# The gates of the last quarter of experts: through a grid in DRAM instead of one-hot products

## The chip, the cores and the metric

The kernel runs on one core of one Trainium2 chip. The metric is the device time of one launch in microseconds. The five engines of the core have queues of their own and wait for each other by semaphores: TensorE (PE, with its weight loads PEld), VectorE (DVE), ScalarE (ACT), GpSimd (POOL) and SyncE (SP), whose queue issues most of the DMAs. DMAs are carried out by 16 DMA engines. SBUF is the memory on the core, PSUM the banks that matmuls write to, DRAM the large memory outside.

## The reference

A decoder of two layers on 256 tokens of width 1024. Each layer has a token mixer (a short convolution in the first, latent attention in the second) and then a PEER mixer, which picks 16 of 16,384 experts for each token and each of 8 heads:

```python
s = einsum("chpd,hpnd->chpn", q, subkeys); top_s, top_i = top_k(s, 16)
cand = top_s[:, :, 0, :, None] + top_s[:, :, 1, None, :]
best_s, best_pos = top_k(cand.reshape(C, 8, 256), 16)
ia = take_along_axis(top_i[:, :, 0], best_pos // 16); ib = take_along_axis(top_i[:, :, 1], best_pos % 16)
expert = ia * 128 + ib
g = softmax(best_s)
act = gelu(einsum("chkd,cd->chk", u_tab[expert], xc)) * g
return einsum("chk,chkd->cd", act, v_tab[expert])
```

An expert has two numbers, ia (first key) and ib (second key), each from 0 to 127. A token has 8 x 16 = 128 chosen experts with a gate g each; two heads may choose the same expert, and then their gates add.

## The kernel before, in words

The kernel gathers no tables. For every expert it computes the product with u for all tokens, and multiplies the gelu by a dense grid of gates, which is zero where a token did not choose the expert. A panel is the 128 experts of one first key: 128 x 1024 values of u or v, 512 KB. There are 128 u panels and 128 v panels in each layer. Products are in split fp32: ScalarE converts a landed panel (`raw`, four slots) to its high part `w_hi` (L944), VectorE (in the selection GpSimd) computes the low part `w_lo` (L1321, L1277), and TensorE multiplies both.

The stages of `peer(l)`: RMS norm (ScalarE's root is L963); the selection, in which VectorE finds the chosen experts while TensorE runs 16 query panels and 6 u panels; "ahead", 26 u panels (j = 0 to 25); "mix", three loops (q = 0, 1, 2) of 8 iterations, each with 4 u panels of the next quarter of first keys and 4 v panels of quarter q; "last", the 32 v panels of the last quarter.

The gates come to the grid by one-hot products. In ahead, `turn(t)` (j = 11 and 13) brings the chosen numbers of each token to lie across partitions; ScalarE copies them to `ia_t`, `ib_t` and the gates to `g32_t`. For 16 tokens at a time VectorE then makes one-hots of the second key (L1538) and of 32 first keys (L1542), multiplies the latter by the high and low halves of the gates (L1547), and TensorE multiplies them token by token into a bank [second key x 32 first keys] (L643, `scatter_side`; L655, `scatter`, in ahead). ScalarE and VectorE bring the result to `arena` (L1015, L1557). Quarter 0 is scattered in ahead, quarters 1, 2 and 3 in the three loops of mix: one group of 16 tokens in each half body. `arena` holds two quarters of the grid, quarter q in half q mod 2. `weigh` (L1572) multiplies gelus by gates for two experts' panels at a time; its semaphore is `w_mul`.

The order of each engine's work is the order of the code. SyncE's queue loads panels: a load waits until the low part of the panel four before is computed (`lo_done`), so the queue is at most four panels ahead. In the first layer GpSimd's queue loads the 56 last rows of the modulation weights (`ada1`, L1301), one at a time, each after VectorE has used the one before (L1347).

Of the kernel before, what the change touches and what calls it, by code (L numbers as in the profile page):

```python
# [20 lines left out]
F32 = mybir.dt.float32  # L21
# [38 lines left out]
SCATTER = 13  # L60
FIRST = KEYS // 8
# [48 lines left out]
def program(nc, xT_in, c_in, pos_in, vec_in, con_in, ada_in, pan_in, key_in, iota_in, u_in, v_in, out):  # L110
    ctx = ExitStack()
    with ctx:
# [80 lines left out]
        smax = sb("smax", [P, 3, 2])  # L193
        ssum = sb("ssum", [P, 3, 2])
        gqk = sb("gqk", [P, 1])[:]
# [12 lines left out]
        eq = [arena[:, a:a + SEL * TOPK].bitcast(BF16) for a in (13312, 3584)]  # L208
        g_high, g_low = [arena[:, a:a + T // 2].bitcast(F16) for a in (6144, 6144 + T // 2)]
# [52 lines left out]
        ada_seen = sem("ada_slot_seen_free")  # L262
# [96 lines left out]
        def _(sp):  # L359
# [16 lines left out]
            def load_experts(l):  # L376
                k0 = KEYS * l
                for i, (kind, n) in enumerate(SEARCH):
                    load(*((pan_in, DENSE[f"peer_q{l}"] + n) if kind == "q" else (u_in, k0 + n)), f"sel{l}", i)
                if l == 0:  # L380
                    sp.dma_start(con[:, C_MASK:C_N], con_in[:, C_MASK:C_N]).then_inc(s_iota, 16)
                    sp.dma_start(iota_w, iota_in).then_inc(s_iota, 16)
                for j in range(AHEAD - EARLY):
                    load(u_in, k0 + EARLY + j, f"ahead{l}", j)
                for q in range(3):
                    with sp.Fori(0, 8) as it:
                        for e in range(4):
                            v = k0 + q * QUART + e
                            load(u_in, it * 4 + (v + AHEAD), f"mix{l}", 64 * q + 2 * e, 8, it)
                            load(v_in, it * 4 + v, f"mix{l}", 64 * q + 2 * e + 1, 8, it)  # L390
                for first in (0, 4):
                    with sp.Fori(first, first + 4) as it:
                        for j in range(4):
                            load(v_in, it * 4 + (k0 + 3 * QUART + j), f"last{l}", j, 4, it)
                    if l == 0 and first == 0:
                        sp.wait_ge(g_done, 2 + 64)
                        sp.dma_start(posi, pos_in.partition_broadcast(P)).then_inc(s_pos, 16)
# [49 lines left out]
        def _(pe):  # L447
# [211 lines left out]
            def peer(l):  # L659
# [33 lines left out]

                for j in range(AHEAD - EARLY):
                    if j in TURN:
                        turn(TURN.index(j))
                    u_panel(l, f"ahead{l}", j, len(SEARCH) + 1 + j, PAN[j % 2])
                    for g in groups_after(j) if j >= SCATTER else ():
                        if g == 1:
                            pe.wait_ge(idx_copied, TT * (l + 1))  # L700
                        scatter(l, g % 2, 64 * l + g + 1)
                for n in range(4):
                    pe.matmul(YB[n][:], zero[:], act_hi[:, 0:512], start=True, stop=False, skip_group_check=True)
                for q in range(3):
                    with pe.Fori(0, 8) as it:
                        for s in range(2):
# [5 lines left out]
                            scatter_side(l, s, it * 2 + (64 * l + 16 * (q + 1) + s + 1))  # L712
# [225 lines left out]
        def _(act):  # L938
# [84 lines left out]
            def peer(l):  # L1023
                rms_of(2 * l + 2)
# [25 lines left out]

                for j in range(AHEAD - EARLY):
                    if j in TURN:
                        turned(TURN.index(j))
                    split_hi(f"ahead{l}", j + HI_LEAD)
# [11 lines left out]
                    for g in groups_after(j) if j >= SCATTER else ():  # L1066
                        copy_gates(0, g % 2, 64 * l + g + 1, g * GT)
# [5 lines left out]
                def mix_body(q, it, end):  # L1073
                        for s in range(2):
# [10 lines left out]
                            copy_first(q + 1, it * 2 + (64 * l + 16 * (q + 1) + s + 1), (it * 2 + s) * GT)  # L1085
# [182 lines left out]
        def _(pool):  # L1268
# [16 lines left out]

            pool.wait_ge(s_const, 48)
# [8 lines left out]
            for j in range(KB):  # L1295
                split_lo("conv_out", j)
            select_panels(0)
            with pool.Fori(0, 96 - ADA_FIRST) as it:
                pool.wait_ge(ada1_used, it + 1)
                pool.sem_inc(ada_seen, 1)  # L1300
                pool.dma_start(ada1[:], ada_in[bass.ds(it + ADA_FIRST, 1)].rearrange("o p n -> p (o n)")  # L1301
                               ).then_inc(ada1_landed, 16)
# [8 lines left out]
            select_panels(1)  # L1311


        @block.vector
        def _(dve):
# [290 lines left out]
            def experts(l):  # L1606
                for j in range(SCATTER, AHEAD - EARLY):
                    for g in groups_after(j):
                        if g % (P // GT) == 0:
                            dve.wait_ge(idx_copied, TT * l + g // (P // GT) + 1)  # L1610
                        second_key_hots(g % 2, 64 * l + g + 1, g * GT)
# [6 lines left out]
                weigh(0, 0, 64 * l + 16 + 2)  # L1618
                split_weighted(0, 64 * l + 1)

                def mix_body(q, it, end):
                    for s in range(2):
# [3 lines left out]
                        second_key_hots(s, it * 2 + (64 * l + 16 * (q + 1) + s + 1), token0)  # L1626
# [10 lines left out]
                        if not (end and s):  # L1637
                            weigh(it * 4 + (2 * s + 2), it * 4 + (q % 2 * QUART + 2 * s + 2), 64 * l + 16 * (q + 1) + 2)
                        split_lo(f"mix{l}", j + 4, 8, it)
                        sum_products(it * 4 + (96 * l + 32 * q + 2 * s + 2), PAN[1], it * 4 + (2 * s + 1))  # L1640
                        add_gates(q + 1, it * 2 + (48 * l + 16 * q + s + 1), token0)
# [16 lines left out]
                def last_body(it, end):  # L1658
                    for s in range(2):
                        split_lo(f"last{l}", 2 * s + 1, 4, it)  # L1660
                        if not (end and s):
                            weigh(it * 4 + (2 * s + 2), it * 4 + (QUART + 2 * s + 2), 64 * l + 64 + 2)
# [369 lines left out]
```

## Time and profile before

| | us |
|---|---|
| median of 3 runs | 1899.36 (1897.52 to 1900.22) |
| the profiled execution, its own time | 1898.04 |
| its span, first to last instruction | 1896.4 |
| TensorE busy | 1879.8 |
| VectorE busy | 1579.3 |
| ScalarE busy | 1023.6 |
| GpSimd busy | 308.3 |

The span is that of one profiled execution; its own time is the span and 1.6 us around it. Busy times of matmuls are modelled, so the chain of waits is read beside them: it goes back from the last instruction to what released each step. In the first layer mix begins at about 299 us and the third loop at about 672; in the second layer the same places lie some 948 us later. HBM is read at 195 GB/s over the span, and 1.05 MB are written.

### The profile page before, as it was taken

The numbers are of one execution on the slowest core, as the hardware profiler recorded it, in microseconds if no ns is written. First come the engines' busy times: TensorE is split into PE (matmuls) and PEld (weight loads), VectorE is DVE, ScalarE is ACT, GpSimd is POOL, SyncE is SP. The second block draws the span as 40 slices with busy tenths as digits, with TensorE's granted clock in tenths as the row PEclk, the third lists the DMA queues.
The fourth block names the chain that finished last, engine by engine and source line by source line (L and its number), as shares of the span: only waits on it lengthen the run. The fifth ranks groups of instructions, "written<-read, shape, count | busy, mean of one in ns | idle before, by whom it ended". The sixth has DMA issues, their size and how long they took to land.

```text
span 1896.4 us, 39962 instructions
## 1 busy us (share of the span) xinstructions
PE 1879.8 (99%) x13150; PEld 1667.1 (88%) x13150; DVE 1579.3 (83%) x3083; ACT 1023.6 (54%) x1658; POOL 308.3 (16%) x177
## 2 busy tenths in 40 slices
PE   9999999999999999999999999999999999999999
PEld 8999998888888888887889999988888888888887
DVE  6758999999999999997765489988888888888866
ACT  4354555555555555554455545555555555555553
POOL 3877500000000000000063574000000000000000
PEclk8999999999999999999999999999999999999999
DMA  9965646777777767777732355456556556556564
GB/s 360 365 209 163 199 133 188 225 229 226 220 228 226 231 224 227 224 229 228 230 107 89 129 161 168 134 169 182 182 177 182 183 179 183 181 179 185 178 191 141
DMA packets 104153, 371.77 MB, mean 196 GB/s; under 512 B 11393, under 2 KB 13825, under 8 KB 103681
## 3 DMA queue, kind: packets, MB, share of 16 engines
q1 hardware_dynamic: 96000, 341.26, 56.7%
q0 software_dynamic: 8064, 29.36, 5.1%
q8 instruction: 52, 0.85, 0.2%
q14 instruction: 37, 0.30, 0.1%
HBM read 369.53 MB, written 1.05 MB: 195 GB/s over the span
## 4 chain that ended last, share of the span: by engine, by line
PE 90%; DVE 5%; ACT 1%; DMA 1%; DVEq 1%; issue 1%; POOL 1%; SPq 0%; ACTq 0%; POOLq 0%
PE bank L624 36%; PE bank L609 17%; PE bank L614 9%; PE bank L588 5%; PE bank L593 5%; PE bank L589 5%; PE bank L643 2%; PE bank L655 1%; DVE w_lo L1321 1%; POOL w_lo L1277 1%; PE bank L671 1%; PE bank L885 1%; DVE arena L1407 1%; PE bank L453 1%; DVE arena L1448 1%
## 5 line engine op out<-in xcount | busy, mean ns | idle before, releaser
L944 ACT CAST w_hi<-raw 128x1024 fp32r<-128x1024 f32 (+1 forms) x603 | 631.2, 1047 | 324.1 <-DMA raw<-in_v_panels 129.4
L1321 DVE TENSOR_TENSOR w_lo<-raw,w_hi 128x1024 fp32r<-128x1024 f32 x488 | 596.8, 1223 | 119.4 <-PE bank L624 52.3
L609 PE MATMUL bank<-act_two,w_hi 128*128 128x512 f32 x1536 | 379.3, 389 | 0.0
L609 PEld LDWEIGHTS bank<-act_two,w_hi 128*128 128x128 f32 x1536 | 288.3, 188 | 59.8
L624 PE MATMUL bank<-w_hi,wt_hi 128*128 128x512 f32 x1024 | 328.0, 401 | 1.4 <-DVE wt_lo L1583 0.8
L624 PE MATMUL bank<-w_lo,wt_hi 128*128 128x512 f32 x1024 | 318.1, 391 | 0.0
L624 PE MATMUL bank<-w_hi,wt_lo 128*128 128x512 f32 x1024 | 317.1, 390 | 0.0
L1277 POOL TENSOR_TENSOR w_lo<-raw,w_hi 128x1024 fp32r<-128x1024 f32 (+2 forms) x115 | 273.6, 2382 | 150.2 <-PE bank L593 54.8
L588 PE MATMUL bank<-act_two,w_hi 128*128 128x256 f32 x984 | 246.1, 288 | 0.0
L589 PE MATMUL bank<-act_two,w_hi 128*128 128x256 f32 x984 | 241.2, 283 | 0.0
L624 PEld LDWEIGHTS bank<-w_hi,wt_lo 128*128 128x128 f32 x1024 | 192.3, 188 | 42.1
L624 PEld LDWEIGHTS bank<-w_lo,wt_hi 128*128 128x128 f32 x1024 | 192.2, 188 | 41.7
L614 PEld LDWEIGHTS bank<-act_two,w_lo 128*128 128x128 f32 x1536 | 209.5, 190 | 15.0
L614 PE MATMUL bank<-act_two,w_lo 128*128 128x256 f32 x1536 | 213.8, 282 | 0.0
L997 ACT COPY ring_g<-bank 128x256 f32 (+1 forms) x192 | 71.7, 374 | 253.9 <-PE bank L614 253.8
L624 PEld LDWEIGHTS bank<-w_hi,wt_hi 128*128 128x128 f32 x1024 | 177.8, 189 | 31.3 <-DVE w_lo L1321 3.6
L589 PEld LDWEIGHTS bank<-act_two,w_hi 128*128 128x128 f32 x984 | 188.5, 192 | 0.0
L588 PEld LDWEIGHTS bank<-act_two,w_hi 128*128 128x128 f32 x984 | 188.2, 191 | 0.0
L1538 DVE TENSOR_TENSOR hot_b<-ib_t,iota 128x2048 bf16<-128x2048 bf16 x128 | 156.0, 1219 | 0.3 <-PE bank L655 0.2
L1301 POOL DMA_DIRECT2D ada<-in_ada_rows x56 | 29.9, 534 | 688.1 <-DVE ada_sum L1347 688.1
L593 PE MATMUL bank<-act_two,w_lo 128*128 128x256 f32 x984 | 138.5, 283 | 0.0
L593 PEld LDWEIGHTS bank<-act_two,w_lo 128*128 128x128 f32 x984 | 127.2, 192 | 0.0
(249 smaller groups left out, 2057.5 us busy)
## 6 DMA issues: line engine op xcount, KB each, us to landing
raw<-in_u_panels SPq DMA_DIRECT2D x256, 512.0 KB, 3.7
raw<-in_v_panels SPq DMA_DIRECT2D x256, 512.0 KB, 3.7
raw<-in_panels SPq DMA_DIRECT2D x81, 512.0 KB, 4.0
ada<-in_ada_rows POOLq DMA_DIRECT2D x56, 512.0 KB, 4.8
arena<-in_ada_rows SPq DMA_DIRECT2D x40, 512.0 KB, 6.6
raw<-in_panels SPq DMA_DIRECT2D x6, 384.0 KB, 3.1
arena<-in_subkeys SPq DMA_DIRECT2D x2, 1024.0 KB, 6.4
xT<-in_xT SPq DMA_DIRECT2D x1, 1024.0 KB, 7.1
```

The costliest lines, as they stand in the source:

```text
L588: pe.matmul(bank, w_hi[:, hi_slot, w], acts[0][k], start=(k == 0), stop=False)
L589: pe.matmul(bank, w_hi[:, hi_slot, w], acts[1][k], start=False, stop=False)
L593: mm = pe.matmul(bank, w_lo[:, lo_slot, w], acts[0][k], start=False, stop=(k == KB - 1))
L609: pe.matmul(bank[:, 0:2 * T], w_hi[:, hi_slot, w], act_two[:, :, a], start=(k == 0), stop=False, skip_group_check=True)
L614: mm = pe.matmul(bank[:, 0:T], w_lo[:, lo_slot, w], act_hi[:, a], start=False, stop=(k == KB - 1), skip_group_check=True)
L624: mm = pe.matmul(YB[2 * t + n][:], wt[:, par, a], (w_hi, w_lo)[v][:, slots[v], n * 512:(n + 1) * 512], start=False, stop=False, skip_group ...
L643: mm = pe.matmul(GB[t // (GT // 2)][:, o:o + 2 * QUART], hb[:, t, :], hg[:, t, :], start=True, stop=True)
L944: nc.scalar.copy(w_hi[:, slot, 0:width], raw[:, slot, 0:width]).then_inc(hi_done, 1)
L997: nc.scalar.copy(ring_g[:, bass.ds(slot * T, T)], bank[:, T:2 * T]).then_inc(lo_copied, 1)
L1277: pool.tensor_tensor(w_lo[:, lo_slot, 0:width], raw[:, slot, 0:width], w_hi[:, slot, 0:width].bitcast(F32), ALU.subtract).then_inc(lo_done, 1)
L1321: dve.tensor_tensor(w_lo[:, lo_slot, 0:width], raw[:, slot, 0:width], w_hi[:, slot, 0:width].bitcast(F32), ALU.subtract).then_inc(lo_done, 1)
L1538: dve.tensor_tensor(wide(hot_b[:, par, :]), each(ib_t, KEYS, token0), numbers(0, KEYS), ALU.is_equal)
```

## The change

The three loops keep quarters 1 and 2 as they are; the one-hots, the scattering, the copies and additions of quarter 3 in the third loop are gone. In their place:

- A grid in DRAM for each layer, 16,384 experts x 256 tokens in fp32. At the start of `peer` ScalarE's queue writes zeros over its last quarter (4.19 MB).
- At j = 15 (`BACK`) of ahead, `turn_back` on TensorE brings ia and ib back to one token a partition, four matmuls; ScalarE (`row_starts`) computes 256 x ib + token and stores the scaled gates in `g32_t`, and VectorE adds 256 x 128 x ia, which gives `place`, the position in the grid.
- GpSimd adds the gates to the grid: one indirect DMA for each of 2 x 8 x 16 columns of `place`, 128 single elements each, with a wait after each head's 32. The gates of all quarters are sent, those of the first three to a part of the grid that nobody reads.
- SyncE waits for the last head's additions ahead of iteration 4 of the third loop, and then loads the last quarter of the grid to `arena` in eight pieces of 512 KB, two ahead of each of the last four iterations' panel loads. VectorE waits for them at the end of the third loop (`s_grid`).
- The 56 rows `ada1` are loaded by SyncE's queue, between panel loads.
- Counts of the semaphores for one-hots and gates follow; `smax`, `ssum` and `gqk` lie in `place`.

```diff
+BACK = 15
@@ sync
+                def load_ada1(it, n):
+                    if l == 0:
+                        sp.wait_ge(ada1_used, it + (n + 1))
+                        sp.dma_start(ada1[:], ada_in[bass.ds(it + (n + ADA_FIRST), 1)].rearrange("o p n -> p (o n)")
+                                     ).then_inc(ada1_landed, 16)
+                def mix_loads(q, it):
+                    for e in range(4):
+                        v = k0 + q * QUART + e
+                        load(u_in, it * 4 + (v + AHEAD), f"mix{l}", 64 * q + 2 * e, 8, it)
+                        load(v_in, it * 4 + v, f"mix{l}", 64 * q + 2 * e + 1, 8, it)
+                        if e % 2:
+                            load_ada1(it * 2, 16 * q + e // 2)
+                def load_grid(n):
+                    a = 3 * QUART + 4 * n
+                    sp.dma_start(arena[:, (QUART + 4 * n) * T:(QUART + 4 * n + 4) * T].rearrange("p (a t) -> p a t", t=T),
+                                 grid[l][a * KEYS * T:(a + 4) * KEYS * T].rearrange("(a p t) o -> p a (t o)", p=P, t=T)
+                                 ).then_inc(s_grid, 16)
-                for q in range(3):
+                for q in range(2):
                     with sp.Fori(0, 8) as it:
...
+                        mix_loads(q, it)
+                with sp.Fori(0, 4) as it:
+                    mix_loads(2, it)
+                sp.wait_ge(added[HEADS - 1], 16 * TT * TOPK * (l + 1))
+                sp.wait_ge(w_mul, 64 * l + 32)
+                for g in range(4):
+                    load_grid(2 * g)
+                    load_grid(2 * g + 1)
+                    mix_loads(2, 4 + g)
@@ tensor
+                def turn_back():
+                    pe.wait_ge(idx_copied, TT * (l + 1))
+                    for n, numbers in enumerate((ia_t, ib_t)):
+                        for t in range(TT):
+                            by_rank = numbers[:, t * P * DUP:(t + 1) * P * DUP].rearrange("p (t r) -> p t r", r=DUP)[:, :, 0]
+                            mm = pe.matmul(SC[0][:, (n * TT + t) * P:(n * TT + t + 1) * P], by_rank, ident_b[:], start=True,
+                                           stop=True)
+                    mm.then_inc(back_done, 1)
...
+                pe.wait_ge(place_ready, l + 1)
...
-                            scatter_side(l, s, it * 2 + (64 * l + 16 * (q + 1) + s + 1))
+                            if q < 2:
+                                scatter_side(l, s, it * 2 + (48 * l + 16 * (q + 1) + s + 1))
@@ scalar
             def peer(l):
+                nc.scalar.dma_start(grid[l][3 * QUART * KEYS * T:KEYS * KEYS * T].rearrange("(p c t) o -> p c (t o)", p=P, t=P),
+                                    zero[:].bitcast(F32).unsqueeze(1).broadcast_to([P, 2 * QUART, P])).then_inc(s_zero, 16)
                 rms_of(2 * l + 2)
...
+                def row_starts():
+                    act.wait_ge(tokens_ready, 1)
+                    act.wait_ge(back_done, l + 1)
+                    for t in range(TT):
+                        i = nc.scalar.activation(row_start[:, t * P:(t + 1) * P], SC[0][:, (TT + t) * P:(TT + t + 1) * P],
+                                                 ACT.Identity, bias=tok[:, t:t + 1], scale=float(T))
+                    i.then_inc(start_ready, 1)
+                    nc.scalar.mul(g32_t[:], gate.rearrange("p t n -> p (t n)"), G_SCALE).then_inc(gates_kept, 1)
@@ gpsimd
+            def add_gates_by_dma(l):
+                pool.wait_ge(s_zero, 16 * (l + 1))
+                pool.wait_ge(place_ready, l + 1)
+                pool.wait_ge(gates_kept, l + 1)
+                for h in range(HEADS):
+                    for t in range(TT):
+                        for k in range(TOPK):
+                            n = t * SEL + h * TOPK + k
+                            pool.indirect_dma_start(grid[l], bass.IndirectOffsetOnAxis(place[:, n:n + 1], 0), g32_t[:, n:n + 1], None,
+                                                    compute_op=ALU.add).then_inc(added[h], 16)
+                    pool.wait_ge(added[h], 16 * TT * TOPK * (l + 1))
@@ vector
+                    if j == BACK:
+                        dve.wait_ge(start_ready, l + 1)
+                        i = dve.scalar_tensor_tensor(out=place[:], in0=SC[0][:, 0:TT * P], scalar=float(KEYS * T),
+                                                     in1=row_start, op0=ALU.mult, op1=ALU.add)
+                        i.then_inc(place_ready, 1)
...
                         if end and s:
+                            if q == 2:
+                                dve.wait_ge(s_grid, 128 * (l + 1))
                             weigh_part(most, (q + 1) % 2 * QUART, w_most)
-                        first_key_hots(q + 1, s, token0)
+                        if q < 2:
+                            first_key_hots(q + 1, s, token0)
```

SyncE's queue at the end of the third loop's rolled part, before the change (first layer; L364 is a panel load, L386 the loop's end, and then come the loads of the last stage):

```order
L364 DMA raw<-in_u_panels 128x1024
L363 REGISTER_ALU
L364 ISA [waits panel_lo_ready]
L364 DMA raw<-in_v_panels 128x1024
L386 REGISTER_ALU
L386 COMPARE_AND_BRANCH
```

And after the change, where the rolled part ends with iteration 3 (L375 is a panel load, L400 an ada row, L414 a piece of the grid):

```order
L375 DMA raw<-in_v_panels 128x1024
L399 REGISTER_ALU
L400 ISA [waits ada1_used]
L400 DMA ada<-in_ada_rows 128x1024
L421 REGISTER_ALU
L421 COMPARE_AND_BRANCH
L414 DMA arena<-gates_by_expert 128x4x256 [waits weighted_gelu_ready,gates_of_head7_added]
L414 DMA arena<-gates_by_expert 128x4x256
L375 DMA raw<-in_u_panels 128x1024 [waits panel_lo_ready]
```

The wait for the additions of all heads now stands ahead of the panel loads of the last four iterations, and two pieces of the grid ahead of each.

GpSimd's queue between the selection of the first layer and the attention's panels, before (L1277 is a low part, L1301 the load of an ada row):

```order
L1277 TENSOR_TENSOR w_lo<-raw,w_hi 128x1024 [waits panel_multiplied,panel_hi_ready] x24
L1298 UNCONDITIONAL_BRANCH
L1298 ISA
L1301 ISA [waits ada1_used]
L1301 DMA ada<-in_ada_rows 128x1024
L1298 REGISTER_ALU
L1298 COMPARE_AND_BRANCH
L1277 TENSOR_TENSOR w_lo<-raw,w_hi 128x1024 [waits panel_multiplied,panel_hi_ready,panel_lo_ready]
```

And after (L1345 is a low part, L1375 one of the additions; the groups of heads 1 to 6 are left out):

```order
L1345 TENSOR_TENSOR w_lo<-raw,w_hi 128x1024 [waits panel_multiplied,panel_hi_ready] x24
L1375 DMA gates_by_expert<-g_t,place 4194304x1 [waits scaled_gates_kept,gate_places_ready,gate_grid_zeroed]
L1375 DMA gates_by_expert<-g_t,place 4194304x1 x31
...
L1375 DMA gates_by_expert<-g_t,place 4194304x1 [waits gates_of_head6_added]
L1375 DMA gates_by_expert<-g_t,place 4194304x1 x31
L1345 TENSOR_TENSOR w_lo<-raw,w_hi 128x1024 [waits panel_hi_ready,panel_multiplied,panel_lo_ready,gates_of_head7_added]
```

A loop of one waiting load has become eight groups of 32 additions, each group behind the landing of the one before.

## Rows read from the trace of the kernel before

**Rows 1.** The page, parts 1 and 2: busy time, 40 slices.
```profile
span 1896.4 us, 39962 instructions
PE 1879.8 (99%) x13150; PEld 1667.1 (88%) x13150; DVE 1579.3 (83%) x3083; ACT 1023.6 (54%) x1658; POOL 308.3 (16%) x177
...
PEclk8999999999999999999999999999999999999999
DMA  9965646777777767777732355456556556556564
GB/s 360 365 209 163 199 133 188 225 229 226 220 228 226 231 224 227 224 229 228 230 107 89 129 161 168 134 169 182 182 177 182 183 179 183 181 179 185 178 191 141
```

**Rows 2.** Chain of waits, 670 to 720 us: start, length, engine, tile, line, number.
```profile
by line: PE bank L624 49.7%; PE bank L609 31.7%; PE bank L614 15.2%; PE bank L643 3.9%
...
680.72 0.48 PE bank L643 x16
681.20 2.83 PE bank L624 x12
...
686.79 2.75 PE bank L624 x12
```

**Rows 3.** Busy time by stretch; its columns are in the first line.
```profile
core 0: us, PE busy (x) PEld busy (x) DVE busy (x) ACT busy (x) POOL busy (x), PEclk, DMA share, GB/s
...
670.00:856.00 186.00, 186.00 (x1155) 159.34 (x1154) 172.60 (x269) 106.40 (x178) 8.48 (x16) 1.00 0.72 226
...
1618.00:1804.00 186.00, 186.00 (x1156) 159.25 (x1155) 155.81 (x227) 105.51 (x178) 0.00 (x0) 1.00 0.59 181
```

**Rows 4.** Timeline, first layer: start, length, engine, line, operation, shapes.
```profile
245.21 2.22 PE L689 MATMUL bank<-ident_b,arena 128*128 128x128 bf16 x32
...
255.51 1.05 ACT L944 CAST w_hi<-raw 128x1024 fp32r<-128x1024 f32 x1
...
255.92 1.22 DVE L1321 TENSOR_TENSOR w_lo<-raw,w_hi 128x1024 fp32r<-128x1024 f32 x1
```

**Rows 5.** Timeline, third loop: a load's issue and its panel's first product.
```profile
752.57 0.33 SPq L364 DMA_DIRECT2D raw<-in_u_panels  x1
...
764.97 1.98 PE L609 MATMUL bank<-act_two,w_hi 128*128 128x512 f32 x8
```

**Rows 6.** Lines L1301, L1277, L1448: instructions, shortest/median/longest ns, starts, forms.
```profile
L1301 POOL DMA_DIRECT2D ada<-in_ada_rows x56: 530/530/722, 219.6 to 937.1; - x56
...
L1277 POOL TENSOR_TENSOR w_lo<-raw,w_hi x115: 1270/2404/3812, 27.5 to 1163.1; 128x1024 fp32r<-128x1024 f32 x105, 128x768 fp32r<-128x768 f32 x6, 128x512 fp32r<-128x512 f32 x4
...
L1448 DVE TENSOR_TENSOR arena<-arena x64: 159/191/2422, 148.3 to 1162.8; 128x32 f32<-128x32 f32 x32, 128x48 f32<-128x48 f32 x16, 128x16 f32<-128x16 f32 x16
```

**Rows 7.** Timeline, selection: GpSimd, and VectorE beside it.
```profile
155.56 2.41 POOL L1277 TENSOR_TENSOR w_lo<-raw,w_hi 128x1024 fp32r<-128x1024 f32 x1 [0.48 <-PE bank L593]
...
156.80 1.53 DVE L1448 TENSOR_TENSOR arena<-arena 128x32 f32<-128x32 f32 x4
```

**Rows 8.** Lines L442, then L364: DMA issue ns, and landing.
```profile
L442 SPq DMA_DIRECT2D out<-xT x4: 372/383/400, 1889.9 to 1893.6; - x4
...
DMA to landing us min/median/max: 2.3/2.3/2.4
...
L364 SPq DMA_DIRECT2D raw<-in_u_panels x256: 327/333/343, 127.5 to 1783.2; - x128
...
DMA to landing us min/median/max: 2.5/3.7/9.4
```

**Rows 9.** Timeline, start of peer in the first layer.
```profile
130.01 0.27 ACT L963 ACTIVATE ring_g<-bank,eps 128x2 f32<-128x2 f32 x1 [1.21 <-PE bank L555]
...
130.38 0.33 SPq L364 DMA_DIRECT2D raw<-in_panels  x1
```

**Rows 10.** Waits, 670 to 856 us: us in total, times, longest.
```profile
ACT w_hi L944 <- DMA raw<-in_v_panels: 23.8, 15, 2.1
```

**Rows 11.** The page, part 3: packets, MB, share of 16 engines.
```profile
q0 software_dynamic: 8064, 29.36, 5.1%
```

More of the change, by code:

```diff
@@ L111, in program @@
     ctx = ExitStack()
+    grid = [nc.dram_tensor(f"gates_by_expert{l}", (KEYS * KEYS * T, 1), F32, kind="Internal").ap() for l in range(2)]
     with ctx:
@@ L192, in program @@
         lat = act32[:, 512:512 + 5 * T]
-        smax = sb("smax", [P, 3, 2])
-        ssum = sb("ssum", [P, 3, 2])
-        gqk = sb("gqk", [P, 1])[:]
+        place = sb("place", [P, TT * SEL], I32)
+        tok = sb("tok", [P, TT])
+        smax, ssum = [place[:, 6 * i:6 * i + 6].bitcast(F32).rearrange("p (e t) -> p e t", e=3) for i in range(2)]
+        gqk = place[:, 12:13].bitcast(F32)
         topv = arena[:, 0:TT * 2 * TOPK]
@@ L261, in program @@
         ada1_used = sem("ada1_used")
-        ada_seen = sem("ada_slot_seen_free")
+        tokens_ready = sem("token_numbers_ready")
+        back_done = sem("expert_numbers_turned_back")
+        start_ready = sem("row_starts_ready")
+        place_ready = sem("gate_places_ready")
+        gates_kept = sem("scaled_gates_kept")
+        s_zero = sem("gate_grid_zeroed")
+        added = [sem(f"gates_of_head{h}_added") for h in range(HEADS)]
+        s_grid = sem("last_quarter_of_gates_landed")
         s_silu = sem("silu_c_ready")
@@ L384, in load_experts @@
                     load(u_in, k0 + EARLY + j, f"ahead{l}", j)
-                for q in range(3):
-                    with sp.Fori(0, 8) as it:
[L387 to L390, printed above, removed]
+                def load_ada1(it, n):
[16 more added lines that the diff above has]
+                for q in range(2):
+                    with sp.Fori(0, 8) as it:
+                        mix_loads(q, it)
[7 more added lines that the diff above has]
+                    mix_loads(2, 4 + g)
                 for first in (0, 4):
@@ L394, in load_experts @@
                             load(v_in, it * 4 + (k0 + 3 * QUART + j), f"last{l}", j, 4, it)
+                        load_ada1(it, 48)
                     if l == 0 and first == 0:
-                        sp.wait_ge(g_done, 2 + 64)
+                        sp.wait_ge(g_done, 2 + 48)
                         sp.dma_start(posi, pos_in.partition_broadcast(P)).then_inc(s_pos, 16)
@@ L696, in peer @@
                         turn(TURN.index(j))
+                    if j == BACK:
+                        turn_back()
                     u_panel(l, f"ahead{l}", j, len(SEARCH) + 1 + j, PAN[j % 2])
@@ L1053, in peer @@
                         turned(TURN.index(j))
+                    if j == BACK:
+                        row_starts()
                     split_hi(f"ahead{l}", j + HI_LEAD)
@@ L1284, in select_panels @@
                     split_lo(f"ahead{l}", j)
+            pool.iota(tok[:], [[P, TT]], 0, 1, allow_small_or_imprecise_dtypes=True).then_inc(tokens_ready, 1)
             pool.wait_ge(s_const, 48)
@@ L1296, in _ @@
                 split_lo("conv_out", j)
-            select_panels(0)
[L1298 to L1302, printed above, removed]
+            def add_gates_by_dma(l):
[9 more added lines that the diff above has]
+                    pool.wait_ge(added[h], 16 * TT * TOPK * (l + 1))
+            select_panels(0)
+            add_gates_by_dma(0)
             pool.wait_ge(lo_done, ring("last0", 31)[3] + RAW)
@@ L1311, in _ @@
             select_panels(1)
+            add_gates_by_dma(1)
         @block.vector
@@ L1625, in mix_body @@
                         split_lo(f"mix{l}", j + 1, 8, it)
-                        second_key_hots(s, it * 2 + (64 * l + 16 * (q + 1) + s + 1), token0)
+                        if q < 2:
+                            second_key_hots(s, it * 2 + (48 * l + 16 * (q + 1) + s + 1), token0)
                         split_lo(f"mix{l}", j + 2, 8, it)
```

20 lines of the change are left out of this document (12 added, 8 removed).

## The prediction

> **What bounds the kernel now.** I read the page first: in a span of 1896.4 us TensorE is busy for 1879.8, at the full clock in all slices but the first; VectorE has 83% [rows 1]. Next the chain of waits in the third loop of the first layer: it never leaves TensorE, and one group of it, L643, is the scattering that the change removes there [rows 2]. The busy time of the third loops says how near the others are: TensorE 186.0 of 186 us in both layers, VectorE 172.6 in the first and 155.8 in the second, DMA engines 0.72 and 0.59 [rows 3]. So TensorE time that is removed in this loop shortens the span one for one, work taken off VectorE and ScalarE there earns nothing, and what is added elsewhere is free until it holds TensorE.
>
> **What is removed.** Each half body of the third loop holds one scatter_side of 16 matmuls. It takes 0.48 us on the chain, and the twelve matmuls behind it take 2.83 us where those not behind one take 2.75 [rows 2]: 0.56 us each. Two layers of 16 make 32, so -17.9 us. The 16 sets of one-hots, gate copies and additions of each layer go too. Nothing is late in their place: TensorE's next wait, for the split panel, is served by a VectorE that has more room than before.
>
> **What is added, step by step.**
> - TensorE: turn_back, four 128x128 bf16 matmuls per layer. The 32 of a turn took 2.22 us [rows 4], so 0.28 us, and with a change of bank 0.35: +0.7 us for both layers.
> - ScalarE: two activations and a multiplication, about 1 us, put ahead of the conversion at 255.51. VectorE: one operation of 256 columns, at most 0.6 us, behind the split at 255.92 [rows 4]. That split serves a panel whose low part TensorE multiplies some 3 us later, so both hide. I take 0; without cover 1.6 us a layer.
> - The zeroing: 4.19 MB written from ScalarE's queue at the start of peer, in runs of 512 bytes. ScalarE idles there for 1.21 us before L963, and SyncE's next load is at 130.38 [rows 9]. The nearest rows are the output stores, also runs of 512 bytes: 383 ns of issue, 2.3 us to landing for 256 KB [rows 8]. At an issue of that size the step is free. I take 0. The other end is the whole transfer: at the 365 GB/s of the second slice [rows 1] 11.5 us, by sixteen stores 37 us.
> - The additions, 256 indirect transfers a layer in eight groups, each group with a wait for its landing. They may start when VectorE has written place, at about 257.2 + 0.6 = 258 us [rows 4]. SyncE waits for the last group ahead of the load that stands at 752.57, whose panel TensorE multiplies at 764.97 [rows 5]. That leaves 495 us. The eight landings at 2.3 us each [rows 8] cost 18, so a transfer may take 1.86 us. The trace has no indirect one. The lower end is GpSimd's plain DMA, 0.53 us, which also has 128 pieces; the upper is GpSimd's longest kind of instruction, 2.40 us at the median [rows 6]. The kind is that of the lower row, but 128 positions must be read and an element added, so I take 1.4: 258 + 256 x 1.4 + 18 = 634 us, and the wait on SyncE is met long before it is reached. Nothing on GpSimd stands behind them that is due earlier, since its next split waits for the end of the last loop.
> - The ada rows move from GpSimd's queue to SyncE's. SyncE would wait there for one VectorE operation that directly follows the split which released the load before, and the load after it needs a later split still. So 0; without that cover each panel load behind a row would come later by that one operation, which its 6 us of room (below) take up.
> - The fetch of the grid: eight loads of 512 KB within four iterations, two at a time ahead of a panel load. Two take 1.05 MB / 365 GB/s = 2.9 us [rows 1]. A panel load has 12.4 us from issue to use [rows 5], of which landing, conversion and split take 3.7 + 1.05 + 1.22 [rows 4, 8]; 6.4 us remain. ScalarE already waits up to 2.1 us for landings without TensorE waiting [rows 10]. I take +1 us for both layers, bounds 0 and 8 x 2.9 = 23.
>
> Sum, against the profiled execution, which took 1898.0 us: 1898.0 - 17.9 + 0.7 + 1.0 = 1881.8. The median of the runs shown is 1.3 us above that execution, so I predict 1883.
>
> **Two rules weighed.** VectorE's L1448 ran 0.16 us at best and 2.42 at worst; its four instructions from 156.80 took 1.53 us because the first waited for a GpSimd instruction that read SBUF until 157.97 [rows 6, 7]. The lock on the shared port is real in this kernel. GpSimd's plain DMAs, issued while VectorE was 92% busy, took 530 ns at the median and 722 at most [rows 6]. The Trainium skill (SBUF — State Buffer, "Who interferes with whom") says that a VectorE instruction with two SBUF inputs contends with a GpSimd instruction that reads SBUF, and that descriptor writing is stopped only by two-port modes. The trace agrees with both; what it cannot show is whether fetching 128 positions counts as a read. It is rival D.
> The Trainium skill (Perfetto Trace Analysis, "DMA Instruction — HWDGE") says that the sequencer is free for its next instruction only after all descriptors of its DMA have been generated, and that a full buffer makes the DMA engines start before that. The trace bears the first half out only at small sizes: 512 pieces cost the queue 383 ns where 128 cost 333 [rows 8]. By the rule the zeroing with 8192 pieces could hold ScalarE; that is rival B.
>
> **Rivals.**
> - A, the additions are late (slower). Place: SyncE's wait in the third loop, behind which stand all panel loads, so TensorE stops when its four panels are used up. It decides from 1.86 us a transfer. The price is 2 x 256 x (x - 1.86): at 2.0 us 72, time 1955; at 2.40, 276, time 2159. For it: nothing in the trace shows an indirect transfer, and each also reads and writes HBM. Against it: 3.5 times the plain DMA would be needed.
> - B, the zeroing holds ScalarE (slower, or no change). ScalarE's root at 130.01 is on TensorE's path, since the norm waits for it. Price 11.5 - 1.2 = 10.3 us a layer, 1883 + 21 = 1904; half of it 1893; at the store's pace 37, 1954.
> - C, the small pieces take the DMA engines. A layer has 32,768 of them, 2048 for each engine. If each took what the mean packet of GpSimd's queue took, 5.1% of 16 x 1896 us over 8064 packets = 192 ns [rows 11], that is 393 us in a window in which 0.72 of 495 is taken: 749 us of work, up to 254 late in the first layer, 190 in the second, about 2330. Against it: that packet carries 4 KB. At half, 96 ns, the sum is 553 and 489 us, 58 late in the first layer only: 1941.
> - D, the additions hold VectorE. In the first layer it has 13.4 us to spare in 186 [rows 3], 26 over the additions' 360 us. If each transfer held it 0.3 us, 77 us, then 51 would show in the first layer and nothing in the second: 1934.
> - E, nothing is gained: the removed blocks were cover for a wait. Time 1899. Against it: the chain has no other engine in it there.
>
> **Chances.** A measurement of this kernel tells a change from none at about 0.2%, 3.8 us. Forecast 0.54, with its own range 1879 to 1890; A 0.12; B 0.15; C 0.09; D 0.05; E 0.05. Faster takes the forecast and a little of B that is only partly held: 0.57. Same takes E and some of B: 0.09. Slower is the rest: 0.34. The range: below 1878 I leave 0.03, and above 1942 about 0.15, which are most of A and the upper part of C. So 1878 to 1942.
>
> **What would show each step.** Right: no L643 in the third loops, each half body 11.0 us in place of 11.6; the 256 transfers start near 258 us and end before 750; SyncE does not wait for them; ScalarE's root at the start of peer comes as soon after TensorE's sums as before. Wrong by A: GpSimd still issuing after 752 us and an idle TensorE in the third loop. By B: TensorE idle at the start of peer, with ScalarE's DMA issue long. By C: panel landings well above 3.7 us and DMA share near 1 from 258 us on. By D: VectorE's instructions longer than their 1.22 and 0.69 us in the first two loops. If TensorE is busy throughout and the time is still above 1890, the removed blocks were worth less than the 0.56 us that I read.

## The result, and the profile after it

The changed kernel takes 2059.53 us (median of 4 runs, 2054.01 to 2063.39), the kernel before 1899.65 in the same comparison: 1.0842 times as long, 95% interval 1.0814 to 1.0869. It is slower by 160 us, where 1883 was forecast. The profiled execution took 2057.83 us with a span of 2056.0.

The page of the changed kernel, to be held against [rows 1]:

```profile
span 2056.0 us, 38401 instructions
PE 1871.7 (91%) x12646; PEld 1659.1 (81%) x12646; DVE 1490.9 (73%) x2893; ACT 1002.0 (49%) x1600; POOL 1239.4 (60%) x634
...
PE   9999999999999980899999999999999999406999
...
POOL 4877288887888887000162772888888888881000
PEclk9999999999999995999999999999999999757999
...
q0 software_dynamic: 73728, 0.29, 8.3%
```

TensorE has fewer busy microseconds than before and yet a share of 91%, because it stands still in two places, slice 16 and slices 35 to 37. They lie in the middle of the two third loops, where the panels of iteration 4 are due. GpSimd is busy with additions up to these places. The waits of TensorE (engine, who it waited for, us in total, times, longest) put a figure on them:

```profile
PE bank L648 <- ACT w_hi L997: 166.4, 2, 98.8
PE bank L512 <- ACT act_two L1024: 2.2, 3, 1.7
```

So 67.6 us in the first layer and 98.8 in the second, and nothing else of size. Behind ScalarE's conversion stands a panel that SyncE had not asked for. SyncE's own queue (start, duration of the issue) in the first layer shows why, beside the last two transfers on GpSimd:

```profile
745.81 0.33 SPq L375 DMA_DIRECT2D raw<-in_v_panels  x1
746.96 0.33 SPq L400 DMA_DIRECT2D ada<-in_ada_rows  x1
820.24 0.94 SPq L414 DMA_DIRECT2D arena<-gates_by_expert  x2
821.24 0.50 SPq L375 DMA_DIRECT2D raw<-in_u_panels  x1
...
815.36 1.55 POOL L1375 DMA_INDIRECT gates_by_expert<-g_t,place  x1 [0.30 <-issue]
817.21 1.55 POOL L1375 DMA_INDIRECT gates_by_expert<-g_t,place  x1 [0.31 <-issue]
```

The panel load that stood at 752.57 before [rows 5] now goes out at 821.24. SyncE goes on 3.0 us after the start of the last addition (817.21 to 820.24), when it has landed, and puts two grid pieces first. The additions were to end at 634. What one of them costs is in the answer on the tile (least, median and greatest ns, then the idle time of GpSimd before them):

```profile
L1375 POOL DMA_INDIRECT gates_by_expert<-g_t,place x512: 1541/1718/2579, 259.1 to 1859.5; - x171
...
  issue: 151.2, 496
  DVE place L1699: 76.7, 2
  DMA gates_by_expert<-g_t,place: 37.6, 14
```

1.54 us at the least, 1.88 in the mean (961.5 us over 512), 0.30 us between any two, and 2.7 us in the mean at each of the 14 waits for a landing. From the first start to the last, 259.13 to 817.21 us, a transfer costs 558.1 / 255 = 2.19 us in the first layer, and (1859.52 - 1270.28) / 255 = 2.31 in the second. In two stretches of the second layer the windows (busy us of each engine, then granted clock, DMA share, GB/s) show TensorE full until SyncE's panels run out:

```profile
1618.00:1760.00 142.00, 142.00 (x801) 121.56 (x800) 102.92 (x140) 77.86 (x127) 120.02 (x56) 1.00 0.73 187
1760.00:1880.00 120.00, 21.21 (x93) 17.69 (x93) 10.82 (x13) 10.05 (x15) 83.78 (x53) 0.57 0.28 39
```

GpSimd needs 120.02 us for 56 transfers (2.14 each) while VectorE works, and 83.78 for 53 (1.58) when VectorE idles. The price is higher beside a working VectorE.

**What sets it.** The timeline of the second layer's third loop, GpSimd's transfers and VectorE's splits of the same microseconds:

```profile
1714.25 2.46 POOL L1375 DMA_INDIRECT gates_by_expert<-g_t,place  x1 [0.30 <-issue]
1717.02 2.44 POOL L1375 DMA_INDIRECT gates_by_expert<-g_t,place  x1 [0.30 <-issue]
1719.76 2.46 POOL L1375 DMA_INDIRECT gates_by_expert<-g_t,place  x1 [0.30 <-issue]
...
1714.07 1.23 DVE L1400 TENSOR_TENSOR w_lo<-raw,w_hi 128x1024 fp32r<-128x1024 f32 x1 [0.63 <-PE bank L653]
...
1716.81 1.23 DVE L1400 TENSOR_TENSOR w_lo<-raw,w_hi 128x1024 fp32r<-128x1024 f32 x1 [0.59 <-PE bank L663]
...
1719.58 1.23 DVE L1400 TENSOR_TENSOR w_lo<-raw,w_hi 128x1024 fp32r<-128x1024 f32 x1 [1.54 <-PE bank L653]
```

The split begins at 1714.07 and ends at 1715.30; the transfer begins inside it, at 1714.25, and ends at 1716.71, which is 1.41 us after the split. The others repeat it. I sorted the 80 transfers that run from 300 to 480 us by the VectorE instruction that runs at their start. Behind L1400 (two SBUF operands, 37 of them) duration minus the rest of that instruction is 1.42 us; behind L1651 and L1617 (also two SBUF operands) 1.38 and 1.42. Those that start beside L1636 (one operand in PSUM, 12 of them) take 1.55 with 0.40 us of it left, the same as the six beside an idle VectorE. So a transfer takes 1.54 us, or 1.42 us from the end of a running VectorE instruction with two SBUF operands, whichever is later. Worked out for all 512 transfers, this rule gives the measured duration within 0.06 us for 497.

In the third loop of the second layer this locks. A transfer that starts 0.18 us into a split waits 1.04, works 1.42, and the next starts 0.30 later: 2.76 us on, where the next split has again just begun, since each product with its split takes 2.75. From 1686 to 1768 us 27 of the 30 transfers take 2.44 to 2.46 us. VectorE's splits pay nothing: L1400 takes 1225 ns in the median, as L1321 does in the kernel before, and a split that starts after a transfer does not wait. The Trainium skill (SBUF — State Buffer, "Who interferes with whom") says that a VectorE instruction with two SBUF inputs contends with a GpSimd instruction that reads SBUF. The trace agrees, and an indirect transfer behaves as such a reader; that it is the reading of the positions which is held up is not shown. Only GpSimd pays here, 0.34 us in the mean.

### The profile page after: what moved, and what is told of

It is laid out like the page before. It is cut to its first block, busy times and chain, and to the rows that moved or that the text cites. A ratio compares the mean times of both kernels' runs of the same rounds, so it can differ in the third digit from the quotient of the medians.

```text
span 2056.0 us, 38401 instructions
## 1 busy us (share of the span) xinstructions
PE 1871.7 (91%) x12646; PEld 1659.1 (81%) x12646; DVE 1490.9 (73%) x2893; ACT 1002.0 (49%) x1600; POOL 1239.4 (60%) x634
## 4 chain that ended last, share of the span: by engine, by line
POOL 46%; PE 32%; issue 8%; DVE 6%; DMA 5%; DVEq 2%; ACT 1%; SPq 0%; ACTq 0%; POOLq 0%
POOL gates_by_expert L1375 45%; PE bank L663 12%; DMA gates_by_expert<-g_t,place 3%; PE bank L627 3%; PE bank L632 3%; PE bank L628 3%; PE bank L648 3%; PE bank L653 1%; DVE w_lo L1400 1%; DVE arena L1527 1%; DMA raw<-in_u_panels 1%; PE bank L512 1%; PE bank L492 1%; DVE arena L1419 1%; DVE arena L1486 1%
## 5 line engine op out<-in xcount | busy, mean ns | idle before, releaser
L1375 POOL DMA_INDIRECT gates_by_expert<-g_t,place x512 | 961.5, 1878 | 265.5 <-issue 151.2
L1400 DVE TENSOR_TENSOR w_lo<-raw,w_hi 128x1024 fp32r<-128x1024 f32 x488 | 596.7, 1223 | 364.0 <-ACT w_hi L997 178.0
L648 PE MATMUL bank<-act_two,w_hi 128*128 128x512 f32 x1536 | 382.9, 392 | 166.4 <-ACT w_hi L997 166.4
L1345 POOL TENSOR_TENSOR w_lo<-raw,w_hi 128x1024 fp32r<-128x1024 f32 (+2 forms) x115 | 272.8, 2375 | 337.9 <-PE bank L663 191.5
L648 PEld LDWEIGHTS bank<-act_two,w_hi 128*128 128x128 f32 x1536 | 290.3, 189 | 227.6 <-issue 167.2
L653 PEld LDWEIGHTS bank<-act_two,w_lo 128*128 128x128 f32 x1536 | 210.6, 191 | 15.2
L653 PE MATMUL bank<-act_two,w_lo 128*128 128x256 f32 x1536 | 214.7, 283 | 0.0
L1617 DVE TENSOR_TENSOR hot_b<-ib_t,iota 128x2048 bf16<-128x2048 bf16 x96 | 117.0, 1218 | 0.2 <-PE bank L694 0.2
```

The costliest lines, as they stand in the source:

```text
L648: pe.matmul(bank[:, 0:2 * T], w_hi[:, hi_slot, w], act_two[:, :, a], start=(k == 0), stop=False, skip_group_check=True)
L653: mm = pe.matmul(bank[:, 0:T], w_lo[:, lo_slot, w], act_hi[:, a], start=False, stop=(k == KB - 1), skip_group_check=True)
L1345: pool.tensor_tensor(w_lo[:, lo_slot, 0:width], raw[:, slot, 0:width], w_hi[:, slot, 0:width].bitcast(F32), ALU.subtract).then_inc(lo_done, 1)
L1375: pool.indirect_dma_start(grid[l], bass.IndirectOffsetOnAxis(place[:, n:n + 1], 0), g32_t[:, n:n + 1], None, compute_op=ALU.add).then_inc( ...
L1400: dve.tensor_tensor(w_lo[:, lo_slot, 0:width], raw[:, slot, 0:width], w_hi[:, slot, 0:width].bitcast(F32), ALU.subtract).then_inc(lo_done, 1)
L1617: dve.tensor_tensor(wide(hot_b[:, par, :]), each(ib_t, KEYS, token0), numbers(0, KEYS), ALU.is_equal)
```

## The experiments

The theory at the start: GpSimd's additions last beyond SyncE's wait, and all else goes as forecast.

**No additions.** The loop over the heads in add_gates_by_dma gets range(0), and SyncE waits for place and the zeroing.

> Left out: all 256 additions of each layer, so the last quarter's gates are zero. Zeroing, turning back, ada rows on SyncE's queue and the fetch of the grid stay. Theory (GpSimd's additions end after SyncE wants them, and nothing else is wrong): TensorE has no idle time in the third loops and the time is the forecast's 1883, within 3 us. Rival (zeroing, fetch or ada rows eat the gain, or the removed blocks were cover for a wait): 1893 to 1900, the same as the kernel before.

Measured: 1884.02 us (1882.68 to 1886.14), ratio 0.9904 (0.989 to 0.9918). Third loops in the windows:

```profile
670.00:856.00 186.00, 184.43 (x931) 156.83 (x930) 135.09 (x182) 100.64 (x151) 0.00 (x0) 1.00 0.80 259
1600.00:1786.00 186.00, 186.00 (x957) 158.87 (x956) 119.45 (x146) 101.03 (x156) 0.00 (x0) 1.00 0.68 212
```

The sum without the additions was right: the removed blocks are worth what was read (a half body of the third loop takes 11.0 us in place of 11.6), and zeroing, fetch and ada rows cost next to nothing. The 1.6 us that TensorE lacks in the first layer are waits for the low part of VectorE's last weighing (1.0, where the kernel before has one of 0.8) and for a split (0.6). That the grid's pieces cause them is not shown; 1 us was forecast for these.

**Half of the additions.** range(HEADS // 2), and SyncE waits for head 3.

> Left out: the additions of heads 4 to 7, so 128 transfers a layer remain. Theory (a transfer costs 2.2 to 2.7 us of GpSimd's time, the end counts and nothing else): the last of them lands near 555 us in the first layer, 195 us before SyncE waits, so 1883 and equal to the kernel without additions within 3 us. Rival (the transfers take DMA engines or SBUF from the others while they run, and so slow TensorE themselves): half of the 176 us lost stays, 1970; at least 5 us above the kernel without additions.

Measured: 1884.24 us (1883.08 to 1885.44), the same as without any. While 128 transfers of 1.92 us run, TensorE loses nothing. What the additions cost is how late the last one is, and nothing else; rivals C and D fall for this kernel.

**Waits one tile behind.**

```diff
     for t in range(TT):
+        if h:
+            pool.wait_ge(added[h - 1][t], 16 * TOPK * (l + 1))
...
-    pool.wait_ge(added[h], 16 * TT * TOPK * (l + 1))
```

> All additions; GpSimd waits, ahead of a head's 16 transfers of one tile, for the head before in the same tile (other tokens can't meet), which landed 35 us ago. Theory (the rate of issue counts most): only the waits for landing go, 7 of 2.8 to 4.2 us in each layer, about 22 us a layer: 68 late becomes 46, 99 becomes 77, so 2059 - 44 = 2015. Rival (the landing waits are what makes it late, and issue would run on in a deeper queue at the cost of a plain transfer): 1883. Rival (the queue then fills and a transfer takes longer): 2059.

Measured: 2033.13 us, ratio 1.0686 (1.0668 to 1.0704): 26 us gained of the 160, not 44. TensorE's two waits fell by 24.4 us:

```profile
PE bank L649 <- ACT w_hi L998: 142.0, 2, 90.0
```

So 52.0 and 90.0 us in place of 67.6 and 98.8. GpSimd no longer waits for a landing, and a transfer still takes 1896 ns in the mean. From 0.30 to 2.7 us a wait adds 2.4, times seven 17 us; the first layer saved 15.6 of them, the second only 8.8. I put that down to VectorE, which sets GpSimd's pace there; no run separates it. My 22 a layer had counted the waits whole. They are a sixth of the loss, the rate is the rest.

**Writes in place of additions.** compute_op=ALU.add is left out of the call.

> Each indirect transfer writes its 128 gates in place of adding them (gates of an expert that two heads choose are then not summed). Theory (the time is GpSimd's, for 128 positions that it reads and turns into pieces; the adding is done later by the DMA engines): a transfer still takes 1.55 us alone and about 1.85 beside VectorE; the landing is shorter by under 2 us, so 2040 to 2060. Rival (the adding makes it slow): a transfer takes 0.5 to 1.2 us, all end before SyncE's wait, 1883.

Measured: 2404.35 us in the median, 2187.72 to 2554.05 over four runs; the trace is of one that took 2409.73. Neither. A transfer became shorter, but from 360 us on, long before SyncE waits for any addition, TensorE, ScalarE and VectorE all but stop (busy us in each stretch, as above):

```profile
258.00:360.00 102.00, 92.82 (x998) 83.90 (x997) 84.87 (x130) 48.45 (x80) 81.05 (x62) 0.98 0.56 166
360.00:540.00 180.00, 36.29 (x113) 23.04 (x113) 16.07 (x23) 8.89 (x14) 133.20 (x136) 0.54 0.08 21
620.00:700.00 80.00, 65.27 (x385) 55.33 (x385) 61.82 (x95) 38.68 (x65) 0.00 (x0) 0.88 0.56 177
```

GpSimd issues a transfer every 1.27 us, the DMA engines are 8% busy with 21 GB/s, and TensorE has 36.29 us of work in 180. When the last transfer is out, at 617 us, the engines go on, and the second layer repeats it. The panel loads are not what is stuck. SyncE issues one at 396.11 us and the next at 469.62, when a slot has come free, and the windows show that each moved its 512 KB within 4 us, with nothing to move in between. TensorE's waits in the whole span and the timeline follow behind the windows:

```profile
396.00:400.00 4.00, 0.42 (x1) 0.29 (x1) 0.25 (x1) 0.00 (x0) 3.09 (x4) 0.50 0.42 132
400.00:469.00 69.00, 4.91 (x12) 3.17 (x11) 2.17 (x4) 3.23 (x6) 50.90 (x53) 0.50 0.02 0
469.00:473.00 4.00, 3.50 (x8) 2.81 (x9) 1.58 (x2) 0.23 (x1) 3.09 (x4) 0.50 0.42 131
...
PE bank L663 <- issue: 166.8, 41, 44.4
PE bank L653 <- issue: 124.6, 29, 33.1
...
421.98 0.37 PE L653 MATMUL bank<-act_two,w_lo 128*128 128x256 f32 x1 [2.43 <-issue]
424.78 0.37 PE L653 MATMUL bank<-act_two,w_lo 128*128 128x256 f32 x1 [2.42 <-issue]
464.40 0.96 POOL L1375 DMA_INDIRECT gates_by_expert<-g_t,place  x1 [0.30 <-issue]
```

TensorE stops in the middle of a product, between two matmuls, and nearly all of its stops are put down to "issue", that is, to nothing that the profile shows. What holds the three engines while the quick writes run stays open.

So the accumulating form costs GpSimd 0.58 us more than the writing one (1.54 against 0.96); my theory that the adding costs GpSimd nothing was wrong.

**The same writes at a slower pace.** A drain and four instructions of 0.1 us stand behind each transfer.

> As e4 (writes in place of additions), with four tiny GpSimd instructions behind each transfer, so that transfers come at 1.9 to 2.4 us in place of 1.27. Theory (in e4 the panel loads got no turn because the transfers followed each other too closely): no idle TensorE before 750 us, panel loads land in 3.6 us, and the time is that of late additions alone, 1884 + 512 x (pace - 1.86), 1905 to 2160 with the pace that the trace shows. Rival (writing single elements to DRAM without adding blocks the loads whatever the pace): TensorE idle from about 370 us on, as in e4.

Measured: 2879.42 us, ratio 1.5145 (1.5087 to 1.5203). The drain held GpSimd for about 3.5 us while the other engines worked, so the pace was 5.6 us, outside of what I had meant; from about 765 us on, with TensorE standing still, it held 1.3 us and the pace was 3.05. But in the stretch in which TensorE had all but stopped beside the quick writes:

```profile
360.00:540.00 180.00, 180.00 (x1113) 154.32 (x1113) 166.63 (x259) 101.99 (x171) 55.36 (x160) 1.00 0.73 225
```

TensorE is full, and its only long waits are the two for the late end, 982.8 us together, which is nearly the whole loss (1884 + 983 = 2867). So writes of single elements do not stop the engines whatever their pace; those every 1.27 us did. The theory's reason, panel loads without a turn, does not fit the trace of the quick writes, and whether it is the pace or the number in flight isn't separated, since the drain changed both.

**64 tokens a transfer.** place[0:64] and g32_t[0:64] in place of all 128 partitions.

> Each of the 256 transfers adds the gates of 64 tokens in place of 128 (tokens 64 to 127 of each tile are left out). Theory (GpSimd pays per position): alone 0.8 to 1.0 us in place of 1.54, beside VectorE 1.2 to 1.4, all end near 700 us, 1884. Rival (it pays per instruction): 1.54 us stays, 2059. Rival (a quick pace keeps the panel loads waiting, as in e4): TensorE idle while GpSimd still adds, above 1900 although the additions end before 752.

Measured: 1976.96 us, ratio 1.0401 (1.0368 to 1.0434). With VectorE idle:

```profile
773.19 1.40 POOL L1375 DMA_INDIRECT gates_by_expert<-g_t,place  x1 [0.30 <-issue]
```

1.40 us for 64 positions, 1.54 for 128. My theory fell here too: the line through both, an estimate from two points, is 1.26 us for the instruction and 0.0022 for a position. In the first layer it helped little (SyncE goes on at 806.65, not 820.24): beside VectorE a transfer now ends 1.27 us behind a running split, and yet the mean from 300 to 480 us is 1.85 us as before. In the second layer TensorE's wait fell from 98.8 to 34.1 us: the shorter transfers fell out of the lock, with a mean of 1.56 us in place of 2.25 from 1670 to 1760. The two waits of 88.8 us give 1884 + 89 = 1973.

**Splits with one SBUF operand.** In the expert loops dve.tensor_copy(w_lo, raw) stands in place of the tensor_tensor of raw and w_hi.

> VectorE's splits of the expert panels become copies of one SBUF operand (the low part is then not raw minus high). Theory (a transfer issued while a VectorE instruction with two SBUF operands runs waits for its end): the splits are 16 of every 24 us of such work, so the mean transfer in the mix loops falls from 1.85 and 2.0 us to 1.6 to 1.75, the additions end some 25 us late in each layer, 1930 to 1975. Rival (the longer transfers are GpSimd's own affair or the DMA's): durations and time stay, 2059. Rival (a copy with one operand holds GpSimd out even more): transfers above 2.0 us and a time above 2059.

Measured: 1984.91 us, ratio 1.0446 (1.0424 to 1.0468), 75 us less than the changed kernel. The mean transfer fell from 1.85 to 1.74 us from 300 to 480 us, from 2.01 to 1.66 from 1300 to 1480, and from 2.25 to 1.68 from 1670 to 1760, where the lock is gone. The direction is the theory's; the time is 10 us above its range. Part of that may be that the copies are not free neighbours either (some transfers that begin beside an idle VectorE took up to 1.94 us when a copy started behind them).

**Later wait, waits one tile behind.** SyncE waits ahead of the last iteration of the third loop, fetches four pieces of the grid there and four in the first two iterations of the last loop; VectorE waits for the first four ahead of its last weighing in the third loop, and for the rest after three iterations of the last.

> As e3, and SyncE waits for the additions 70 us later, ahead of the last iteration of the third loop; half of the grid is fetched there, half in the first two iterations of the last loop. Theory (only the distance of the last addition from SyncE's wait counts): in the first layer the additions end near 811, the wait stands near 822, nothing late; in the second they end 563 us + 29 after their start (34 transfers now beside VectorE at 0.85 us more), about 30 late: 1884 + 30 = 1914. Rival (the fetch so late makes VectorE wait for its pieces): 5 us or more on top, and VectorE idle on arena before its weighing.

Measured: 1933.02 us, ratio 1.0172 (1.0153 to 1.0191). The one long wait of TensorE that is left:

```profile
PE bank L663 <- ACT w_hi L1012: 43.8, 1, 43.8
```

It is in the second layer; the first is hidden as expected. 43.8 in place of 30: 1884 + 44 = 1928, near the profiled span of 1927.4. In the second layer 602 us pass from the first addition's start to the last one's, where 592 were expected; that is most of the difference. Moving the end and moving the deadline come to the same.

**Less by the grid.** Two versions that are meant to be of use. In the first only the first tile's tokens (128 of 256) go by the grid in both layers, with the wait where it was; the others are scattered in iterations 4 to 7 of the third loop. In the second the later wait of above, both tiles in the first layer and one in the second:

```diff
+BY_GRID = (1, 1)        # second version: (2, 1)
...
-                            if q < 2:
+                            if q < 2 or first and BY_GRID[l] == 1:     # first: 0 or 4, the loop's start
                                 scatter_side(...)
...
-                    for t in range(TT):
+                    for t in range(BY_GRID[l]):
                         for k in range(TOPK):
```

> Only the first 128 tokens' gates go by the grid (128 transfers a layer), the other 128 tokens are scattered in iterations 4 to 7 of the third loop, as before. Theory: the additions end near 569 us, 180 before the wait; 16 of the 32 removed blocks are back at 0.56 us: 1884 + 9 = 1893, 0.995 of the kernel before. Rival (a removed block is worth something only where all are gone): 1900, ratio 1.

Measured: 1896.71 us (1890.47 to 1899.1, ten runs), ratio 0.9972 (0.996 to 0.9984). Faster than before, by 4 us where 8 were expected; its profiled span of 1892.6 has no long wait. What is missing goes with the granted clock: the two runs with a mean of 0.995 took 1890.47 and 1892.44, 8.6 us less than the seven of the kernel before with the same mean (1900.07), and the other eight have 0.990 to 0.994. Why its clock is lower in most runs isn't settled.

> The later wait and fetch of e6; all 256 transfers in the first layer, 128 in the second, whose other 128 tokens are scattered as before. Theory: nothing is late in either layer, 8 of the 32 removed blocks are back: 1884 + 4.5 = 1888.5, 0.993 of the kernel before. Rival (the later fetch costs): 1893 or more.

Measured: 1890.03 us, ratio 0.9936 (0.992 to 0.9953): 11 us faster than the kernel before and 170 faster than the change as it stood. Its last transfer of the first layer ends ahead of SyncE's first piece of the grid, and TensorE's longest wait in the whole span is 2.5 us:

```profile
809.07 1.60 POOL L1400 DMA_INDIRECT gates_by_expert<-g_t,place  x1 [0.30 <-issue]
...
813.91 0.39 SPq L421 DMA_DIRECT2D arena<-gates_by_expert  x1
```


## Why the prediction was wrong, step by step

- **What bounds the kernel**: right. TensorE's time is the kernel's time: the kernel without additions gains what the blocks took on TensorE, and nothing for the work taken from VectorE and ScalarE can be seen.
- **The removed blocks**, -17.9 us: right. Without the additions the kernel is 18.6 us below the kernel before of the same comparison; the whole sum said 16.2.
- **turn_back, ScalarE's and VectorE's additions, the ada rows**: right in sum, within what a run of this kernel can tell; no run takes one of them alone.
- **The zeroing** at nothing: right. The queue holds ScalarE's place for 0.60 us and the root comes 1.21 us behind TensorE's sums as before [rows 9]; rival B did not happen:

```profile
129.27 0.60 ACTq L1077 DMA_DIRECT2D gates_by_expert<-zero  x1
130.89 0.26 ACT L1016 ACTIVATE ring_g<-bank,eps 128x2 f32<-128x2 f32 x1 [1.21 <-PE bank L594]
```

- **The start of the additions** at 258 us: right, 259.13.
- **The additions, 1.4 us each**: this step failed, and with it the sum. The limit of 1.86 was worked out well; the price beside it was a choice between 0.53 and 2.40 that leaned on the lower row, and three things were missing in it. The instruction by itself is 1.54 us, not 1.4. The 0.30 us between two instructions of one queue was left out, though it is what the sum needs. And 0.34 us in the mean for VectorE's hold was weighed as rival D only in the direction in which VectorE pays. 1.54 + 0.34 + 0.30 = 2.18 us a transfer. With VectorE silent it would have been 1.84 by this sum, an estimate that lies right at the limit; the hold is what put it clearly beyond.
- **The wait for eight landings**, 2.3 us each: measured 2.7, a small miss.
- **Rival A** is what happened, at a chance of 0.12. Its formula holds. Without the 19 us of landing waits x is 539 / 255 = 2.11 in the first layer and 570 / 255 = 2.24 in the second; 256 x (2.11 - 1.86) + 256 x (2.24 - 1.86) = 64 + 97 us, and the trace has 67.6 + 98.8. 1884 + 166 = 2050. Of the last 9 us about half is the clock. Eight matmuls of L648 take 3.76 us directly behind the first standstill, where eight of the kind take 1.98 in the kernel without additions; behind the second they take 3.78, and the eight of L653 after them 1.91 in place of 1.12. By the starts of these groups that is some 1.8 and 2.8 us, an estimate; the rest is not split up. The granted clock of the stretch from 764 to 870 us is 0.68, a mean of the two levels of 1.2 and 2.4 GHz; TensorE had stood idle for 67.63 us before these matmuls. Here the changed kernel:

```profile
828.55 3.76 PE L648 MATMUL bank<-act_two,w_hi 128*128 128x512 f32 x8 [67.63 <-ACT w_hi L997]
```

and the kernel without additions:

```profile
765.63 1.98 PE L649 MATMUL bank<-act_two,w_hi 128*128 128x512 f32 x8
```

The range ended at 1942, which is A at 1.97 us a transfer. A price of which only 0.53 and 2.40 are known, with a limit of 1.86 in between, should not have had a chance of only 0.12 for the far side: 0.29 of the interval lay there.

- **Rival D** had a slip in its sum: by its own rows the second layer has 30.2 us to spare in 186, 58 over 360 us, so 77 - 58 = 18 us would show there too, and its time is 1952, not 1934. It changes nothing here: VectorE's splits took what they took before.

## What to carry to other kernels

Where work moves to a queue with a deadline, work out the limit per piece first, and if the trace has no such piece, spread the chance over the interval in proportion, gap between instructions included. A wait is worth what the last piece misses it by: half of the pieces cost nothing at all here, and all of them 160 us. So fit the amount to the window, or move the wait toward the first use, before giving up the idea.

## What was new of the hardware

- An indirect accumulating transfer of 128 single elements holds GpSimd for 1.54 us, of 64 elements for 1.40, and without accumulation for 0.96; 0.30 us lie between two. With accumulation it lands 2.8 us after its start at the least and 3.6 in the median.
- Such a transfer waits for the end of a running VectorE instruction with two SBUF operands and takes 1.42 us from there; one with an operand in PSUM does not hold it. Two such loops can lock: 2.44 to 2.46 us per transfer in place of 1.54. Transfers of 64 elements fell out of the lock.
- Beside indirect writes every 1.27 us TensorE, ScalarE and VectorE all but stopped (36.29 us of TensorE's work in 180), with the DMA engines 8% busy and SyncE's 512 KB loads moved within 4 us of their issue; additions every 2.2 us and writes every 5.6 us stopped nothing. What holds the engines is not known.
- A DMA of 4.19 MB in pieces of 512 bytes held the issuing queue for 0.60 us at most and landed in 22.4 at most.
